# Three exponential and low-half steps of a hybrid mLSTM + GLA layer, placed elsewhere in ScalarE's, GpSimd's and VectorE's queues

## What is computed

```
h = _rmsnorm(x, g_norm1) * (1.0 + scale1) + shift1
z = h @ w_in
...
ha, C1, n1, m1 = _mlstm(qa, ka, va, ig, lf, C0, n0, m0)
la = (log_sigmoid(lr_b @ w_alpha + b_alpha) / GLA_TAU)
hb, S1 = _gla(qb, kb, vb, la, S0)
...
y = (sigmoid(g_a) * ha + sigmoid(g_b) * hb) @ w_out
x = x + gate1 * y
ffn = (silu(h2 @ w_ffn_gate) * (h2 @ w_ffn_up)) @ w_ffn_down
```

## Time and profile before

| | |
|---|---|
| median of 3 runs | 1853.44 us (1852.53 to 2180.71) |
| the profiled execution | 1853.46 us |
| its span | 1851.7 us |
| TensorE busy | 1815.7 us (98%) |
| VectorE, GpSimd, ScalarE busy | 1133.4, 776.4, 732.3 us |
| granted TensorE clock, mean | 0.997 |

### The profile page before, as it was taken

The page is one execution under the profiler, slowest core; times in us unless marked ns, Lnnn a source line. Parts: engine busy times, 40 slices in busy tenths (PEclk is TensorE's granted clock), DMA queues, the critical chain, the costliest instruction groups (busy, mean ns, idle before and its releaser), DMA issues.

```text
span 1851.7 us, 36566 instructions
## 1 busy us (share of the span) xinstructions
PE 1815.7 (98%) x14652; PEld 1742.7 (94%) x14652; DVE 1133.4 (61%) x1960; ACT 732.3 (40%) x1528; POOL 776.4 (42%) x667
## 2 busy tenths in 40 slices
PE   7999999999999999999999999999999999999998
PEld 5899999999999999999989899989999999999998
DVE  6852746526474364753575688885675667566656
ACT  4543435344353443544435544223223222322327
POOL 4241434423344233432344773244345444544545
PEclk9999999999999999999999999999999999999999
DMA  9332231422224222232243741111112011111212
GB/s 314 118 98 58 78 92 53 137 63 78 87 58 130 64 83 82 58 122 66 83 140 96 216 127 57 46 46 51 43 46 69 26 58 56 58 35 46 69 47 95
DMA packets 182640, 154.82 MB, mean 84 GB/s; under 512 B 10324, under 2 KB 163092, under 8 KB 181960
## 3 DMA queue, kind: packets, MB, share of 16 engines
q1 hardware_dynamic: 182170, 152.27, 27.1%
q10 hardware_dynamic: 302, 0.22, 0.0%
HBM read 130.96 MB, written 21.50 MB: 82 GB/s over the span
## 4 chain that ended last, share of the span: by engine, by line
PE 80%; DVE 9%; POOL 3%; issue 3%; ACT 2%; DMA 2%; SPq 0%; ACTq 0%; DVEq 0%; POOLq 0%
PE bank L1076 24%; PE bank L2485 20%; PE bank L2454 12%; PE bank L1098 9%; PE bank L1243 3%; PE bank L2352 3%; PE bank L2319 1%; PE bank L1315 1%; POOL mix L1650 1%; PE bank L1223 1%; DVE gate L1906 1%; DVE y_rows L2918 1%; DMA x_rows<-in_w_ada 1%; PE bank L1296 1%; DVE y_rows L3099 1%
## 5 line engine op out<-in xcount | busy, mean ns | idle before, releaser
L1076 PE MATMUL bank<-h_hi,w_by_parity 128*128 128x320 f32 (+2 forms) x2304 | 449.0, 328 | 1.9 <-POOL w_by_parity L1574 1.9
L1574 POOL TENSOR_TENSOR w_by_parity<-w_raw,w_by_parity 128x512 fp32r<-128x512 f32 x128 | 193.3, 1510 | 530.0 <-ACT w_by_parity L1331 530.0
L1076 PEld LDWEIGHTS bank<-h_hi,w_by_parity 128*128 128x128 f32 x2304 | 378.1, 189 | 16.5 <-issue 11.2
L1076 PE MATMUL bank<-h_lo,w_by_parity 128*128 128x384 f32 (+2 forms) x1152 | 233.5, 324 | 0.0
L2784 POOL TENSOR_TENSOR f_by_parity<-w_raw,f_by_parity 128x512 fp32r<-128x512 f32 x107 | 145.7, 1367 | 196.1 <-ACT f_by_parity L2549 196.0
L2784 POOL TENSOR_TENSOR w_by_parity<-w_raw,w_by_parity 128x512 fp32r<-128x512 f32 x107 | 143.6, 1348 | 149.8 <-ACT w_by_parity L2549 149.8
L1076 PEld LDWEIGHTS bank<-h_lo,w_by_parity 128*128 128x128 f32 x1152 | 194.8, 189 | 0.0
L3133 DVE SCALAR_TENSOR_TENSOR x_t<-bank,ada,x_t 128x352 f32<-128x352 f32 (+1 forms) x288 | 155.8, 568 | 56.8 <-PE bank L2454 38.8
L1098 PE MATMUL bank<-w_by_parity,h_hi 128*128 128x256 f32 x1024 | 170.1, 281 | 1.0 <-POOL w_by_parity L1574 1.0
L2454 PE MATMUL bank<-act_hi,f_by_parity 128*128 128x352 f32 x528 | 155.0, 325 | 1.5 <-POOL act_lo L2818 1.1
L2454 PE MATMUL bank<-act_hi,w_by_parity 128*128 128x352 f32 x528 | 154.1, 323 | 1.4 <-DVE ffn_temps L2918 1.2
(11 more groups left out here) (570 smaller groups left out, 3779.9 us busy)
## 6 DMA issues: line engine op xcount, KB each, us to landing
w_raw<-in_w_in SPq DMA_DIRECT2D x128, 256.0 KB, 3.0
w_ada_tile<-in_w_ada SPq DMA_DIRECT2D x32, 512.0 KB, 4.2
w_raw<-in_w_out SPq DMA_DIRECT2D x48, 256.0 KB, 2.9
w_raw<-in_w_ffn_gate SPq DMA_DIRECT2D x44, 256.0 KB, 3.0
w_raw<-in_w_ffn_up SPq DMA_DIRECT2D x44, 256.0 KB, 3.0
w_raw<-in_w_ffn_down SPq DMA_DIRECT2D x44, 256.0 KB, 2.8
w_ada_ring<-in_w_ada SPq DMA_DIRECT2D x10, 512.0 KB, 9.6
x_scratch<-x_turned_rows SPq DMA_DIRECT2D x1, 4224.0 KB, 16.4
```

What stands on the lines that cost most here:

```text
L1076: last = pe.matmul(g.ps[b][:, 0:n], slice_k(x[:, s], k), y[:, 4 * h + k, c0:c0 + n], start=(h == 0 and k == 0 and m == 0), stop=(h == 1 an ...
L1574: pool.tensor_tensor(lo, by_parity(raw[:, r]), hi.bitcast(F32), ALU.subtract).then_inc(s_lo, 1)
```

## The change

Three things, in three places of the program:

1. `rows_exp` goes from slot 17 to slot 18 of S, so that on ScalarE it stands behind the split of v0's second half.
2. `decay` keeps VectorE's part at slot 1 of A; ScalarE's two exponentials become a stage of their own, `decay_exp`, at slot 3, behind that slot's split and evacuation (and, for head 0, behind `alpha_hi`).
3. In B the low half of the first pair of value chunks is subtracted by VectorE, behind the low half of the keys, and counted on `s_rlo`; GpSimd keeps the other three pairs.

```
-    "S": [("rows", 8), ("conv_q", 16), ("taps_q", 16), ("rows_exp", 17), ("silu_q", 19), ...
+    "S": [("rows", 8), ("conv_q", 16), ("taps_q", 16), ("rows_exp", 18), ("silu_q", 19), ...
-    "A": [("decay", 1), ("ada_load0", 2), ("alpha_hi", 3), ("values_split", 7), ...
+    "A": [("decay", 1), ("ada_load0", 2), ("alpha_hi", 3), ("decay_exp", 3), ("values_split", 7), ...
...
+        def values_lo(e, i, c, done):
+            e.wait_ge(s_rhi, hi_of_b(i, "values", c))
+            e.tensor_tensor(values_lo_of(c, 2), V[1][:, c:c + 2, 0:DV],
+                            values_hi_of(c, 2).rearrange("p (c d) -> p c d", d=DV).bitcast(F32), ALU.subtract).then_inc(done, 1)
...
-                            pe.wait_ge(s_vlo, vlo_of_b(i, c))
-                            if c == 0:
-                                pe.wait_ge(s_rlo, rlo_of_b(i, "keys"))
+                            if c < 2:
+                                pe.wait_ge(s_rlo, rlo_of_b(i, "values"))
+                            else:
+                                pe.wait_ge(s_vlo, vlo_of_b(i, c))
...
-                    elif name == "decay":
+                    elif name == "decay_exp":
                         act.wait_ge(s_warg, i + 1)
...
-                        for c in range(0, NC, 2):
-                            pool.wait_ge(s_rhi, hi_of_b(i, "values", c))
-                            pool.tensor_tensor(values_lo_of(c, 2), ...).then_inc(s_vlo, 1)
+                        for c in range(2, NC, 2):
+                            values_lo(pool, i, c, s_vlo)
...
                         dve.tensor_tensor(keys_lo[:, 0:SEQ], KD[:, 0:SEQ], keys_hi_b[:, 0:SEQ].bitcast(F32), ALU.subtract).then_inc(s_rlo, 1)
+                        values_lo(dve, i, 0, s_rlo)
```

More of the change, by code:

```diff
@@ L608 @@
 AT_SLOT = {
-    "S": [("rows", 8), ("conv_q", 16), ("taps_q", 16), ("rows_exp", 17), ("silu_q", 19), ("vs0", 20), ("rows_t", 21), ("conv_k", 23),
+    "S": [("rows", 8), ("conv_q", 16), ("taps_q", 16), ("rows_exp", 18), ("silu_q", 19), ("vs0", 20), ("rows_t", 21), ("conv_k", 23),
           ("taps_k", 24), ("silu_k", 25), ("decay_load", 25), ("interq_load", 25), ("vs1", 26), ("vsum", 27)],
-    "A": [("decay", 1), ("ada_load0", 2), ("alpha_hi", 3), ("values_split", 7), ("scores", 8), ("keys", 8), ("vs0", 8), ("interq", 8), ("alpha_lo", 9),
+    "A": [("decay", 1), ("ada_load0", 2), ("alpha_hi", 3), ("decay_exp", 3), ("values_split", 7), ("scores", 8), ("keys", 8), ("vs0", 8), ("interq", 8), ("alpha_lo", 9),
           ("masked", 9), ("recurrence_split", 9), ("chunk0", 13), ("ada_load1", 13), ("chunk1", 14), ("ada0", 14), ("vs1", 14),
@@ L832, in mixer_phase @@
                                         + {"scores": 1, "queries": 2, "keys": 3, "values": 4 + c // 2, "state": 4 + NC // 2 + c}[what])
[L833 to L836, removed]
+        rlo_of = lambda i, what, c=0: i * (2 * (NC + 2) + 1) + {"keys": 1, "scores": 2, "queries": 3, "state": 4 + c}[what]
+        rlo_of_b = lambda i, what, c=0: i * (2 * (NC + 2) + 1) + NC + 2 + {"scores": 1, "queries": 2, "keys": 3, "values": 4, "state": 5 + c}[what]
+        vlo_of = lambda i: i * (NC // 2) + 1
+        vlo_of_b = lambda i, c: vlo_of(i) + c // 2
         s_adl = sem("ada_tile_loaded")
@@ L1616, in window @@
                     elif name == "values_split" and isB(w):
-                        for c in range(0, NC, 2):
-                            pool.wait_ge(s_rhi, hi_of_b(i, "values", c))
-                            pool.tensor_tensor(values_lo_of(c, 2), V[1][:, c:c + 2, 0:DV],
-                                               values_hi_of(c, 2).rearrange("p (c d) -> p c d", d=DV).bitcast(F32), ALU.subtract).then_inc(s_vlo, 1)
+                        for c in range(2, NC, 2):
+                            values_lo(pool, i, c, s_vlo)
                     elif name == "values_split":
```

## The result

| | before | after |
|---|---|---|
| median of 20 runs | 1852.38 us | 1855.24 us |
| ratio of the medians, 95% interval | | 1.0015 [1.0008, 1.0021] |
| the profiled execution, its span | 1853.46, 1851.7 us | 1856.45, 1854.7 us |

One of the 20 executions of the kernel before (2180.71 us) was a slow one; the ratio is that of the fast ones. The change costs 2.8 us (1.5 to 3.9 by the interval), 0.15%. That is far inside 2%. So I read stretches between marks instead: the starts of TensorE's matmuls in this table.

The account below looks back on a forecast made before the run. TensorE was taken to bound the kernel, with at most 36 us in its waits. From 1853.46, the three parts' +0.8, 0 and +1.7 gave 1856.0 us, range 1851.5 to 1858.0.

Parts of the forecast that it names:

- What bounds: TensorE busy 1815.7 of 1851.7 us; the change aims at 3.5 us of its waits in S and B.
- Edit 1, +0.8: Window S: moving `rows_exp` removes two waits of 2.35 us, but TensorE waits at vsum for VectorE's longer chain; +0.8 us.
- The first turn: Window S: GpSimd's earlier low half goes ahead of VectorE's L1985, delaying it and all behind by 1.1 us.
- Later turns: Window S: GpSimd's later splits still push VectorE's chain, but give 0.3 us back.
- the turn at 98.83: Window S: this GpSimd split moves to about 96, into small VectorE operations, costing 0.7 instead of 0.9 to 1.0 us.
- the last turn: Window S: GpSimd's split ahead of L1710 still pushes an operation of VectorE's chain; no size of its own.
- Edit 2, 0: A windows: `decay_exp` delays q's second bank from 122.74 to 123.8, but TensorE does not wait; 0 us, bound +0.2 in A0.
- Edit 3, +0.57 for each window: Three B windows: chunk0's wait goes, but VectorE's L1906 ends later and delays the second state product; +1.7 us in all.
- The sum: Whole kernel: 1853.46 + 0.8 + 0 + 1.7 = 1856.0 us.
- The clock (0.02): Rival, chance 0.02: the 3.4 us wait at vsum lets TensorE's clock fall, costing 1.7 us; total 1857.7.

Follow-up runs that it names:

- e1: Only `rows_exp` moved to slot 18 of S, against the kernel before: 1854.17 us, ratio 1.0005.
- e4: `rows_exp` at slot 18, GpSimd's low half of v0's second half held until VectorE's rows chain ended (L1987), against the kernel before: 1854.18 us, ratio 1.0005.
- e9: `rows_exp` at slot 18, GpSimd's low half held until VectorE hands q's convolution to ScalarE's tanh, against the kernel before: v0 to vsum 26.12 us; no total given.
- e2: Only `decay_exp` made its own stage at slot 3 of A, against the kernel before: 1853.86 us, ratio 1.0005.
- e3: Only the first value pair's low half in B moved from GpSimd to VectorE, against the kernel before: 1852.06 us, ratio 1.0000.
- e6: First pair's low half in B on VectorE, GpSimd's other three pairs held until L1906 is done, against the kernel before: 1849.53 us, ratio 0.9988.
- e5: `rows_exp` at slot 18 and vsum two pieces later (slot 29 of S), against the kernel before: 1848.18 us, ratio 0.9981.
- e8: All three parts, vsum at slot 29, GpSimd's low half held past the rows' chain, its B pairs until L1906, against the kernel before: 1844.77 us, ratio 0.9964.
- e12: Repeat of `rows_exp` alone at slot 18, against the kernel before: 1851.01 us, a single time.

## Why the prediction was right, and where not

**What bounds.** Right. The waits lay where I said, and what comes last behind each place is VectorE (L1715, L1864), as the waits after show.

**Edit 1, +0.8.** The wait at vsum is 2.9 us (3.09 on the weight load's row) where I had 3.4, and vsum is 0.68 us later in the changed kernel, 0.69 in e1. The first turn costs the 1.1 us that I took from VectorE's rows. Later turns were to give 0.3 of it back, and the traces give about 0.6: the turn at 98.83 cost 0.92 and now falls on a small operation, 0.57 us instead of 0.16, and the last turn costs 0.15 less. The chain itself is 0.52 longer; TensorE's mark moved 0.17 against it. The Trainium skill's "SBUF — State Buffer", section "Who interferes with whom", has VectorE and GpSimd exclude each other there, and e4 and e9 agree: the turn is paid in full or falls into a gap. The same section has tensor_scalar among the operations that can take that pair; by this too the trace agrees, since e4's TENSOR_SCALAR paid 0.86 us.

**Edit 2, 0.** Right, by e2: q's second bank starts at 124.12, which is 123.82 without this execution's offset of 0.30 (I had 123.8), and the A windows did not move.

**Edit 3, +0.57 for each window.** +0.55, +0.46, +0.63 in the changed kernel and +0.51, +0.46, +0.64 in e3. The path was right row by row: L1912 at 2.25 us, L1864 at 1.28, the wait of 1.2 us. The Trainium skill's warning about moving operations between these two engines ("Perfetto Trace Analysis", section "Optimizing Scalar/DVE Operations") agrees with e3, which gained nothing, but not with e6, in which the same move gains: it is the turns that cost, and their order can be chosen.

**The sum.** 1856.0 was right in the size of the change: +2.5 forecast, +2.8 measured. That it also lies within 0.5 us of the profiled execution (1856.45) is luck, since that one holds a start that is 1.08 us later, a fall of the clock for 1.55 and an unchanged rest of the program that is 1.94 shorter. And the sum was right with a term missing, the rival "The clock (0.02)". I sized it well, 1.7 us against 1.3 to 1.6 (once 2.65), and gave it almost no chance, because a stretch with 2.1 us of waits showed 1.00. Those 2.1 us were two waits, of 0.4 and 1.7 us, with matmuls in between, and the new one is a single wait of 3 us, which I had even computed. The same trace had the nearer example, and I did not look at it: behind the single wait of 2.01 us at 961.70 the clock is at 0.50. The term's fair place was in the sum, at about 0.9 us; the marks then say 0.68 + 0.9 + 1.64 = 3.2, inside the interval, and so is my 2.5. The measurement does not tell these two apart; the traces do.

**What stays open.** The marks (v0 of S to the adaLN matmuls in A3, without what a fall in S cost) and the timed runs (by their ratios), both in us against the kernel before:

| | after | e1 | e2 | e3 | e4 | e5 | e6 | e8 |
|---|---|---|---|---|---|---|---|---|
| marks | +2.3 | +0.6 | +0.3 | +1.6 | +0.6 | -2.3 | -2.5 | -5.3 |
| timed runs | +2.8 | +0.9 | +0.9 | 0.0 | +0.9 | -3.5 | -2.2 | -6.7 |

Each difference taken alone lies within its interval or at its edge, but the three that exceed 1 us (e3, e5, e8) all lie below. The timed runs carry no trace, but they do have a mean granted clock: 0.9979 in e3 and 0.9982 in e8, against 0.9969 and 0.9973 in the kernel before beside them. One fall, some 3 us at 0.50 in 1852, makes about 0.001 of that mean and 1.5 us, which is the size of both gaps; fewer falls in their timed runs than in those of the kernel before would explain them. Against it stands e1, whose mean is 0.0007 higher without a lower time, and e5, where it is 0.0003 higher; and a mean does not say where the clock fell. So this is argued and not shown. Nor do I know why e1's clock held where that of e12, the same code, fell.

## What to carry to other kernels

Before moving work off one of two engines that exclude each other, look at what the other one is in the middle of at the new time: a low half that starts 6 us earlier is only free if it lands in a gap of the engine it takes turns with, and holding it for one instruction merely passes the bill on. Where TensorE's wait is traded for another further on, move the waiting matmul behind the next piece of independent work as well (here two slots, 2.4 us), and before merging two short waits into one long one, count what the clock did behind single waits of that length elsewhere in the same trace (here 2.01 us at 961.70). To price a wait, read the weight load's row too, not the matmul's alone.

## What I had not expected of the hardware

- TensorE's granted clock was 0.50 for about 3 us behind a single wait of 2.8 to 3.1 us in 6 of 7 executions, once for twice as long. Where the price can be read off (five of them) it was 1.3 to 2.65 us, about half of the wait over again or more. Behind a wait of 2.0 us it was 0.50 in 6 of 13, at 1.5 us each.
- A GpSimd subtraction of 128x512 delays a VectorE TENSOR_SCALAR, which has one tensor input, by 0.86 us (0.84 to 1.70, e4), nearly as much as an operation with two (1.09).
- The first matmul behind a wait takes 0.1 us longer, and its idle time reads 0.2 to 0.3 us shorter than that of the weight load beside it; removing 0.56 us of waits by the matmul rows gave 0.82 back (e6).
